# Windowed attention in units of eight heads, on alternating halves of the TensorE array

## What is computed

```
q = (x @ w_q).reshape(B, nb, BLOCK, N_KV_HEADS, GROUP, HEAD_DIM)
kv = (x @ w_kv).reshape(B, S, 2, N_KV_HEADS, HEAD_DIM)
...
scores = jnp.einsum('bnqgrd,bnkgd->bngrqk', q, kb) * (HEAD_DIM ** -0.5)
scores = jnp.where(valid, scores - slopes * dist, NEG_BIG)
m = jnp.maximum(jnp.max(scores, -1, keepdims=True), sink_l)
p = jnp.exp(scores - m)
probs = p / (jnp.sum(p, -1, keepdims=True) + jnp.exp(sink_l - m))
out = jnp.einsum('bngrqk,bnkgd->bnqgrd', probs, vb)
return out.reshape(B, S, N_HEADS * HEAD_DIM) @ w_o
```

## Time and profile before

| | us |
|---|---|
| median of 3 runs (3003.4 to 3004.99) | 3003.65 |
| the profiled execution's own time | 3003.5 |
| its span in the trace | 3001.1 |
| TensorE busy (96% of the span) | 2876.8 |
| VectorE busy (55%) | 1640.7 |
| ScalarE busy (25%) | 749.3 |
| GpSimd busy (30%) | 911.8 |

### The profile page before, as it was taken

One profiled execution on the slowest core, in us unless ns is written; L12 is line 12 of the kernel. 1 busy time (PEld: TensorE's weight loads), 2 busy tenths in 40 slices (PEclk: granted clock), 3 DMA queues, 4 the chain that ended last, 5 costly groups with the idle time before them and its releaser, 6 DMA issues.

```text
span 3001.1 us, 36000 instructions
## 1 busy us (share of the span) xinstructions
PE 2876.8 (96%) x14070; PEld 2347.4 (78%) x14070; DVE 1640.7 (55%) x2612; ACT 749.3 (25%) x1717; POOL 911.8 (30%) x798
## 2 busy tenths in 40 slices
PE   8999959999999999999899899899999999999995
PEld 7888848788888888888788544487888888888884
DVE  3699974744444444444730599727444444444457
ACT  3212343221111111222111466502222111111131
POOL 3354502232233233232132333323223223223323
PEclk9999979999999999999999899999999999999998
DMA  4000003111111111111221000021111111111111
GB/s 131 29 18 25 28 1 119 29 43 31 40 43 39 33 43 43 36 43 36 71 78 32 22 1 1 23 94 36 43 36 40 31 43 43 36 36 43 43 36 70
DMA packets 158644, 124.65 MB, mean 42 GB/s; under 512 B 27905, under 2 KB 135801, under 8 KB 158488
## 3 DMA queue, kind: packets, MB, share of 16 engines
q1 hardware_dynamic: 149640, 96.83, 11.3%
q10 hardware_dynamic: 8848, 25.69, 2.3%
HBM read 112.01 MB, written 10.49 MB: 41 GB/s over the span
## 4 chain that ended last, share of the span: by engine, by line
PE 86%; DVE 9%; ACT 3%; issue 1%; DMA 0%; POOL 0%; POOLq 0%; ACTq 0%; SPq 0%; DVEq 0%
PE bank L588 26%; PE bank L593 26%; PE bank L591 26%; PE bank L953 3%; PE bank L929 2%; DVE conv_acc L1293 2%; PE bank L944 1%; DVE stats L1223 1%; DVE y L1241 1%; DVE x_lo L1249 1%; ACT y L1094 1%; DVE y L1236 1%; DVE y L1451 1%; PE bank L618 1%; ACT probs L1187 1%
## 5 line engine op out<-in xcount | busy, mean ns | idle before, releaser
L588 PE MATMUL bank<-x_hi,w_hi 128*128 128x512 f32 (+1 forms) x2688 | 957.2, 356 | 3.8 <-DVE x_lo L1249 1.6
L591 PE MATMUL bank<-x_lo,w_hi 128*128 128x512 f32 (+1 forms) x2688 | 953.4, 355 | 0.0
L593 PE MATMUL bank<-x_hi,w_lo 128*128 128x512 f32 (+1 forms) x2688 | 953.3, 355 | 0.0
L514 POOL CAST w_hi<-raw_pieces 128x512 fp32r<-128x512 f32 x348 | 329.9, 948 | 1802.9 <-issue 1363.8
L588 PEld LDWEIGHTS bank<-x_hi,w_hi 128*128 128x128 f32 x2688 | 509.5, 190 | 79.0 <-POOL w_lo L518 6.3
L591 PEld LDWEIGHTS bank<-x_lo,w_hi 128*128 128x128 f32 x2688 | 509.5, 190 | 70.6
L593 PEld LDWEIGHTS bank<-x_hi,w_lo 128*128 128x128 f32 x2688 | 509.1, 189 | 70.8
L518 POOL TENSOR_TENSOR w_lo<-raw_pieces,w_hi 128x512 fp32r<-128x512 f32 x348 | 472.2, 1357 | 27.9
L1451 DVE TENSOR_TENSOR y<-y,bank 128x512 f32<-128x512 f32 x440 | 296.2, 684 | 200.5 <-PE bank L593 198.5
L1412 DVE SCALAR_TENSOR_TENSOR gate_conv<-bank,ffn_conv_table,gate_conv 128x510 f32<-128x510 f32 x132 | 86.2, 653 | 373.5 <-ACT up_conv L1125 371.5
L1293 DVE SCALAR_TENSOR_TENSOR conv_acc<-glu,conv_table,conv_acc 128x1024 f32<-128x1024 f32 (+1 forms) x310 | 257.6, 906 | 35.4 <-ACT conv_acc L1034 35.4
(11 more groups left out here) (144 smaller groups left out, 3765.5 us busy)
## 6 DMA issues: line engine op xcount, KB each, us to landing
raw_pieces<-in_ffn_w_up_dram SPq DMA_DIRECT2D x168, 256.0 KB, 2.9
raw_pieces<-in_ffn_w_down_dram SPq DMA_DIRECT2D x84, 256.0 KB, 2.6
raw_pieces<-in_conv_w_pw_dram SPq DMA_DIRECT2D x48, 256.0 KB, 2.7
y<-in_x_prompt_dram ACTq DMA_DIRECT2D x16, 512.0 KB, 6.8
residual_dram<-y ACTq DMA_DIRECT2D x10, 512.0 KB, 2.6
y<-residual_dram ACTq DMA_DIRECT2D x10, 512.0 KB, 10.7
out_dram<-y SPq DMA_DIRECT2D x10, 512.0 KB, 2.6
raw_pieces<-in_attn_w_q_dram SPq DMA_DIRECT2D x32, 128.0 KB, 2.4
```

The source lines that it names most:

```text
L514: pool.tensor_copy(WH[:, p % RING, :], raw[:, p % RAW, :]).then_inc(piece_hi, 1)
L588: mm = pe.matmul(out, left[0], right[0], start=first, stop=False)
L591: pe.matmul(out, left[0], right[1], start=False, stop=False)
L593: return pe.matmul(out, left[1], right[0], start=False, stop=last)
```

## The change

The list `ATT` now has 20 units (n, rr) of eight heads, both groups of rr, and the first four stand in the order (0, 0), (1, 0), (0, 1), (1, 1). What follows from it:

- Scores alternate: head r of the first half of the array into bank 0 or 6, head r of the second half into bank 1 or 7. The values of the two groups alternate too and write partitions 0 to 63 and 64 to 127 of one bank, bank 5. High and low parts are taken from all 128 partitions at once.
- The transposes of a unit fill banks 2, 3 and 4 in turn, and each group of four waits for the copy of three groups ago. `probs_T` has two pairs of slots: one in storage of its own, the other in the first two slots of `raw`. The last two units use storage of `q_sb` in their place.
- Each head has one more column, the sink, which ScalarE writes there (`set_sink`). Maximum, exponential and row sum go over it, so the four small steps on the sink are gone from VectorE and the exponential of the sink from ScalarE. The maximum is one instruction of all eight heads that also negates.
- VectorE scales three heads of a unit, GpSimd five.
- Scores of unit 0 stand behind Q tile 5 and those of unit 1 behind Q tile 6; exponentials of units 0 and 1 stand behind ScalarE's copies of Q tiles 6 and 7.
- On TensorE two of the four score pairs of unit i + 3 stand ahead of the values of unit i, and two behind. ScalarE does exponentials two units ahead instead of three.
- The third buffer of `probs` and `probs_T` lie in the storage of `w_lo`. So no output weight is split before the last scaling, and SyncE loads none before the values of unit 17 are done.

The diff, cut to its core. Most removed lines are left out: they are those of the functions printed above.

```diff
@@ -127,19 +128,31 @@
...
+        with ExitStack() as a:
+            probs_third = sb("probs_third", [P, HEADS, 3 * P + 1], where=a)
+            probs_T = sb("probs_T", [P, 2, GROUP * P], where=a)
...
+            probs_two = sb("probs", [P, 2, HEADS, 3 * P + 1], where=a)
+            v_sb = sb("v", [P, TT, KVD], where=a)
+            k_sb = sb("k", [P, NKV // 2, T], where=a)
         chan = sb("channel_table", [P, 5, KT])
 
...
@@ -302,6 +305,42 @@
...
+        ATT = [(0, 0), (1, 0), (0, 1), (1, 1)] + [(n, rr) for n in range(2, TT) for rr in range(2)]
+        def key_blocks(n):
+            lo, hi = (0, T0) if n < T0 else (T0, TT)
+            return range(max(lo, n - 1), min(hi, n + 2))
+        KEYS_TO = [sum(len(key_blocks(n)) for n, _ in ATT[:i]) for i in range(len(ATT) + 1)]
+        SCORE_BANKS = ((0, 1), (6, 7))
+        AV_BANK = 5
+        DVE_HEADS = 3
+        LAST_UNITS = len(ATT) - 2
+        def probs_of(i):
+            return probs_two[:, i % 3] if i % 3 < 2 else probs_third[:]
+        def score_columns(n):
+            return slice((3 - len(key_blocks(n))) * P, 3 * P)
+        def probs_T_pair(i, j):
+            return (KEYS_TO[i] + j) % 2 + (2 if i >= LAST_UNITS else 0)
+        def probs_T_slot(i, j, par):
+            pair = probs_T_pair(i, j)
+            if pair == 0:
+                return probs_T[:, par, :].rearrange("p (r t) -> p r t", t=P)
+            if pair == 1:
+                return raw[:, par, :].rearrange("p (r t) -> p r t", t=P)
+            return q_sb[:, GROUP * par:GROUP * (par + 1), cols(pair - 2)]
+        PAIRS = [probs_T_pair(i, j) for i, (n, _) in enumerate(ATT) for j in range(len(key_blocks(n)))]
+        def pair_used_before(u):
+            return max([w + 1 for w in range(u) if PAIRS[w] == PAIRS[u]], default=0)
...
@@ -405,6 +444,7 @@
+            sp.wait_ge(av_done, KEYS_TO[LAST_UNITS])
             for n in range(2):
...
@@ -546,13 +577,12 @@
+            def normalise_part(i):
                 pool.wait_ge(recip_ready, i + 1)
-                for r in range(GROUP // 2, GROUP):
-                    ins = pool.tensor_scalar(probs[:, b, r, 0:nk], probs[:, b, r, 0:nk], srec[:, b, r:r + 1],
-                                             None, ALU.mult)
+                for h in range(DVE_HEADS, HEADS):
+                    part = probs_of(i)[:, h, score_columns(ATT[i][0])]
+                    ins = pool.tensor_scalar(part, part, srec[:, i % 3, h:h + 1], None, ALU.mult)
                 ins.then_inc(probs_ready_pool, 1)
...
@@ -566,10 +596,10 @@
             for i in range(len(ATT)):
-                if i < RING - 1:
-                    stretch(B_O + i, B_O + i + 1)
-                normalise_half(i)
-            stretch(B_O + RING - 1, B_FFN1)
+                normalise_part(i)
+            pool.wait_ge(probs_turned, 2 * KEYS_TO[LAST_UNITS])
+            pool.wait_ge(av_done, KEYS_TO[LAST_UNITS])
+            stretch(B_O, B_FFN1)
...
@@ -913,46 +943,65 @@
...
+            def scores(i, heads):
+                n, rr = ATT[i]
+                kb = key_blocks(n)
+                for r in heads:
+                    q = GROUP * i + r
+                    if q >= 2:
+                        pe.wait_ge(score_kept, 2 * (q - 1))
+                    for par in range(2):
+                        half = slice(par * HD, (par + 1) * HD)
+                        pe.matmul(bank[SCORE_BANKS[q % 2][par]][:, 0:len(kb) * P], q_sb[half, GROUP * rr + r, cols(n)],
+                                  k_sb[half, rr, kb[0] * P:(kb[-1] + 1) * P], start=True, stop=True
+                                  ).then_inc(score_done, 1)
+            def turn_probs(i):
+                pe.wait_ge(probs_ready, i + 1)
+                pe.wait_ge(probs_ready_pool, i + 1)
+                n, rr = ATT[i]
+                c0 = score_columns(n).start
+                for j in range(len(key_blocks(n))):
+                    for par in range(2):
+                        u = 2 * (KEYS_TO[i] + j) + par
+                        if u >= 3:
+                            pe.wait_ge(probs_T_kept, u - 2)
+                        for r in range(GROUP):
+                            mm = pe.transpose(bank[2 + u % 3][:, cols(r)],
+                                              probs_of(i)[:, GROUP * par + r, c0 + j * P:c0 + (j + 1) * P], ident[:])
+                        mm.then_inc(probs_turned, 1)
+            def values(i):
+                n, rr = ATT[i]
+                kb = key_blocks(n)
+                if i >= 1:
+                    pe.wait_ge(av_lo, i)
+                for j, b in enumerate(kb):
+                    pe.wait_ge(probs_T_kept, 2 * (KEYS_TO[i] + j + 1))
+                    for par in range(2):
+                        g = 2 * rr + par
+                        mm = pe.matmul(bank[AV_BANK][par * HD:(par + 1) * HD, :], v_sb[:, b, g * HD:(g + 1) * HD],
+                                       probs_T_slot(i, j, par), start=(j == 0), stop=(j == len(kb) - 1))
+                    mm.then_inc(av_done, 1)
+            kept_to = []
             for c in range(KT):
                 for ch in range(3):
                     channel_projection(B_Q + 2 * c, ch)
+                kept_to.append(unit)
+                if c in (KT - 3, KT - 2):
+                    if c == KT - 3:
+                        pe.wait_ge(qkv_kept, kept_to[GROUP - 1])
+                    scores(c - (KT - 3), range(GROUP))
             pe.wait_ge(qkv_kept, unit)
+            scores(2, range(GROUP))
+            for i in range(len(ATT)):
+                turn_probs(i)
                 if i + 3 < len(ATT):
+                    scores(i + 3, range(2))
+                values(i)
+                if i + 3 < len(ATT):
+                    scores(i + 3, range(2, GROUP))
 
             pe.wait_ge(av_lo, len(ATT))
             out_projection(B_O, 1)
@@ -1175,34 +1224,59 @@
...
+            def set_sink(i):
+                rr = ATT[i][1]
+                act.activation(probs_of(i)[:, :, 3 * P], sink[:, HEADS * rr:HEADS * (rr + 1)], ACT.Copy
+                               ).then_inc(sink_set, 1)
+            def exponentials(i):
+                n, rr = ATT[i]
+                act.wait_ge(max_ready, i + 1)
+                for h in range(HEADS):
+                    part = probs_of(i)[:, h, score_columns(n).start:3 * P + 1]
+                    ins = act.activation(part, part, ACT.Exp, bias=nmax[:, i % 3, h:h + 1],
+                                         accum_out=ssum[:, i % 3, h:h + 1])
+                ins.then_inc(exp_ready, 1)
+            def keep_turned(i):
+                for j in range(len(key_blocks(ATT[i][0]))):
+                    for par in range(2):
+                        u = 2 * (KEYS_TO[i] + j) + par
+                        act.wait_ge(probs_turned, u + 1)
+                        if par == 0 and pair_used_before(u // 2):
+                            act.wait_ge(av_done, pair_used_before(u // 2))
+                        act.activation(probs_T_slot(i, j, par),
+                                       bank[2 + u % 3][:].rearrange("p (r t) -> p r t", t=P), ACT.Copy
+                                       ).then_inc(probs_T_kept, 1)
+            def heads_high(i):
+                n, rr = ATT[i]
+                act.wait_ge(av_done, KEYS_TO[i + 1])
+                act.activation(XH[:, GROUP * rr:GROUP * (rr + 1), cols(n)],
+                               bank[AV_BANK][:].rearrange("p (k t) -> p k t", t=P), ACT.Copy).then_inc(av_hi, 1)
+            set_sink(0)
+            set_sink(1)
             for c in range(KT):
                 for c0, n in CHUNKS:
                     keep(q_sb[:, c, c0:c0 + n], n, scale=HD ** -0.5)
+                if c >= KT - 2:
+                    exponentials(c - (KT - 2))
+            set_sink(2)
+            act.wait_ge(exp_ready, 2)
+            set_sink(3)
+            set_sink(4)
+            act.wait_ge(piece_split, B_O)
+            for i in range(len(ATT)):
+                if i >= 1:
+                    heads_high(i - 1)
+                keep_turned(i)
+                if i + 2 < len(ATT):
+                    exponentials(i + 2)
+                    if i + 5 < len(ATT):
+                        act.wait_ge(exp_ready, i + 3)
+                        set_sink(i + 5)
+            heads_high(len(ATT) - 1)
 
             act.wait_ge(av_lo, len(ATT))
             for t in range(TT):
@@ -1521,62 +1595,55 @@
...
+                n, rr = ATT[i]
                 kb = key_blocks(n)
+                nk, d0 = len(kb) * P, (kb[0] - n + 1) * P
                 if i >= 3:
+                    dve.wait_ge(probs_turned, 2 * KEYS_TO[i - 2])
                 for r in range(GROUP):
+                    for par in range(2):
+                        q, h = GROUP * i + r, GROUP * par + r
+                        dve.wait_ge(score_done, 2 * q + par + 1)
+                        dve.scalar_tensor_tensor(out=probs_of(i)[:, h, score_columns(n)], in0=dist[:, d0:d0 + nk],
```

(20 more changed lines are left out.)

124 lines of the change are left out of this document (12 added, 112 removed).

## The result

The kernel after takes 2931.02 us (median of 4 runs, 2930.31 to 2931.59), the kernel before took 3004.32 on the same chip (3003.4 to 3006.73): a ratio of 0.9758, 95% interval 0.9744 to 0.9772. The profiled execution has a span of 2929.8 us against 3001.1. The stage from the last Q tile to the output projection takes 200.0 us against 273.3.

What follows compares the result with a forecast made beforehand. TensorE alone was taken to bound the long middle of the 273.3 us attention stage. Five pieces sum to 221.0, a gain of 52, less 7 for clock falls: 3003.5 - 45 = 2958 us, range 2936 to 2990.

Steps and rivals of the forecast that it cites:

- (a): Among the Q tiles: scores of two units now stand there, 3.2 us for the small, 4.3 for the large, 7.5 added.
- (b): From the last Q product to ScalarE's copy of unit 1, through exponentials, reciprocal, GpSimd and transposes: 15.8 us.
- (c): Turns of units 1 to 13: nine at 12.3, one at 10.5, one at 11.9, two at 11.0: 155.1 us.
- (d): Three small (two-block) units at 8.3 us each, a loop that goes over two units: 24.9 us.
- (e): Tail: last exponentials, GpSimd on the last two units, transposes, copy, values, high and low parts: 17.7 us.
- The stagger: TensorE's scores and values on alternating array halves: n products take n + 1 record times, not 2n.
- ScalarE's hand-offs: ScalarE's sink (0.3 us) and high part (0.6) behind the exponentials, in the 12.3 us loop of a large unit.
- The clock term: Four falls of TensorE's clock in the 12 large units, about 1.7 us each: 7 us off the gain.
- pairs in series: Rival: the halves' products run one after the other, middle at 14.2 us, stage 255, gain 18: 2985 us; chance 0.18.
- The clock did not stay down: Rival: idle gaps keep the attention stage at 1.2 GHz, stage 330 us: 3060 us, slower; chance 0.07.
- extra waits: Rival: one value bank and doubled hand-offs add two us per large unit, eating the gain: 3005 us; chance 0.08.
- VectorE's scaling stands still beside GpSimd's: Rival: each of VectorE's three scaling steps waits for a GpSimd one of 1.35 us: 2982 us; chance 0.05.

Runs made afterwards that it cites:

- the runs of one half: Kernel after with score products, or in a second run value products, of both groups on partitions 0 to 63 only: 2950.5 and 2949.2 us.
- three pairs and the early reciprocal: Kernel after with a third pair of slots for transposed probabilities and VectorE's reciprocal moved ahead of the next scores' maximum: 2909.9 us, ratio 0.9693.

## Why the prediction was wrong in size

The place, the loop and its members were right; the terms of the loop were too large. ScalarE waits for values in the middle of its copies, the output weights are hidden, VectorE's three small steps are gone. The sum was 221.0 us for five pieces and is 207.2, with three falls of the clock in it.

| piece | predicted | measured |
|---|---|---|
| (a) added among the Q tiles | 7.5 | 7.17 |
| (b) to unit 1's first copy | 15.8 | 15.08 |
| (c) units 1 to 13 | 155.1 | 145.24 |
| (d) three small units | 24.9 | 22.19 |
| (e) tail | 17.7 | 17.50 |
| clock, on top | 7 | about 4.6, inside (c) and (e) |

- **The stagger** is the step that failed in kind, and the large unit (12.3 predicted, 11.37 measured) is the term that it made too large. "n products take n + 1 record times": they take n. The records start in pairs, one of each half 0.007 us apart, and two pairs of scores are four steps, a first of 0.43 and three of 0.32 us (1.49 in all, predicted 1.7), the values of a block two (1.03 and 0.09 to the copy, predicted 1.55). That is 0.64 of the 0.9 us by which the large unit was overrated. The run with the halves in another order shows that neighbours need not even differ (1.50 us). That the halves overlap at all was a choice between two ends which no row of the kernel before decided; the runs of one half decide it, 2.77 against 1.49 us for the scores and 1.90 against 1.03 for the values.
- **ScalarE's hand-offs** are the next: sink and high part 0.9 predicted, 0.61 on the chain, since the high part runs into the copies behind it. Transposes 2.27 (2.15), copies 1.09 and exponentials 4.79 were right. 2.27 + 1.49 + 1.12 + 1.09 + 4.79 + 0.61 = 11.37.
- **The clock term**, 7 us for four falls in large units, was added on top of the sum. There were three falls, one in a large unit (unit 1), one in unit 2 and one in the tail, at about 4.6 us together, and none in units 4 to 13. A fall costs 1.6 us in a large unit (1.7 predicted). Why units 4 to 13 have none is not shown. In units 4 to 9 TensorE waits 0.71 and 1.21 us in two pieces; with one piece of 1.96, made by moving one 0.2 us instruction of VectorE, there were five, and with three pairs of slots a piece of 2.04 brought none. So the forecast knew the price and not the number. The low end, 2936, stood for no falls and somewhat shorter loops; no stagger in any of the units and what came outside the stage went past it by 5 us.
- **The small units** were overrated by 0.9 each. The terms of their loop measured less: GpSimd's five heads take 4.71 us (5.0), transposes 1.97 (2.3), two pairs of scores 1.06 (1.25), values 1.87 (2.25).
- **Outside the stage** nothing was predicted, and 5.2 us came: 2.8 ahead of the Q tiles, within what the runs of one program differ by, and 2.4 behind, of which 2 repeat.

Together: 9.9 + 2.7 + 0.7 + 0.3 + 0.2 = 13.8 for the pieces, 7 for the clock, 5.2 outside, on a forecast of 45: 71, and the spans differ by 71.3. As the pieces measured hold about 4.6 us of falls, the share of each cause is rather 18.4 for the loops and ends without a fall, 2.4 for the clock and 5.2 outside.

Of the rivals, pairs in series gives 2972 on the chip (predicted 2985): 13.75 a large unit and not 14.2. The clock did not stay down (0.98 over the stage), and no 2 us a unit came from extra waits; that rival's sum, 24 on 2985, is 3009 and not the 3005 written.

The rival that VectorE's scaling stands still beside GpSimd's is half right, and the prediction's reading against it, a mean of 0.58 us in the earlier trace rows, hid that. Taken one by one in the kernel after, the first two scalings of a unit on VectorE and the first on GpSimd are:

```profile
1739.39 0.42 DVE L1626 TENSOR_SCALAR probs<-probs,one_over_sum 128x384 f32<-128x384 f32 x1
1739.72 0.74 DVE L1626 TENSOR_SCALAR probs<-probs,one_over_sum 128x384 f32<-128x384 f32 x1
1739.45 1.47 POOL L585 TENSOR_SCALAR probs<-probs,one_over_sum 128x384 f32<-128x384 f32 x1 [4.93 <-DVE one_over_sum L1622]
```

A scaling that VectorE starts before GpSimd's first takes 0.42 us, the others 0.74, in the kernel before as well (24 and 24 of its 48 of 128 x 384); GpSimd's take 1.24 alone and up to 1.47 beside them. With three pairs and the early reciprocal GpSimd is already at work when VectorE comes to the first of its three, and in ten of eleven such units that one takes 0.74 to 0.75 too. So each slows the other, VectorE by 0.32 us and GpSimd by up to 0.23, and neither stands still for the whole of the other's instruction (at least 1.24 us for GpSimd's, 0.42 for VectorE's). The mean of 0.64 against 0.58 is two slow ones in three instead of one in two.

## What to carry to other kernels

Where a trace shows products of two halves side by side, as here (eight score records in 1.49 us against 2.77 of one half), count record times of the busier half and, for products of this kind, nothing for a stagger, then look at once for the loop that takes over: here it was a pair of slots (a third pair gave 11 us), then a reciprocal behind a maximum (10 more). Neither the sum of TensorE's waits in a unit nor their longest piece told here whether the clock would fall: a unit with the same waits kept it or lost it. So every edit that starts one engine earlier is to be measured with the granted clock beside it, and the time at a granted clock of 0.50 belongs in the table of results, or its cost (here 1.6 us for a fall in a large unit) is put down to the edit. And look at the single durations behind a mean when two engines share work (here 0.42 and 0.74 us behind 0.58 and 0.64). Where the granted clock falls in some units and not in others, repeating a product into its own bank inside a wait is a cheap test, and tells what the clock costs (here five falls in large units became none, and the stage 5.2 us shorter).
